# Attention scores with 128 contracted rows: query parts stacked, keys doubled, two matmuls in place of three

## The reference, cut to what matters

```python
C_NA = 1024; NA_HEADS = 16; NA_HEAD_DIM = 64        # 16 heads of 64 channels
scale = dh ** -0.5                                   # 0.125
s_g = jnp.einsum('bhnqd,bhrnkd->bhnqrk', qb, kb).astype(f32) * scale
s_g = s_g + bias.transpose(0, 2, 3, 1, 4)[None]
s_g = jnp.where(mask[:, :, None, :], s_g, NEG_INF)
s_x = jnp.einsum('bhnqd,bhmd->bhnqm', qb, k_m).astype(f32) * scale + mb[None, :, None, None, :]
s = jnp.concatenate([s_g.reshape(B, H, ncb, NA_QB, kh * NA_KU), s_x], axis=-1)
p = jax.nn.softmax(s, axis=-1).astype(v.dtype)
```

## Time and profile before

| what | us |
|---|---|
| median of 3 runs | 1200.71 (1199.37 to 1201.31) |
| profiled execution | 1199.38 |
| its span in the trace | 1197.6 |
| PE busy | 1144.7 (96% of the span) |
| DVE busy | 756.7 (63%) |
| ACT busy | 551.2 (46%) |

### The profile page before, as it was taken

One profiled execution on the slowest core, in us unless ns is written; L12 is line 12 of the kernel. 1 busy time (PEld: TensorE's weight loads), 2 busy tenths in 40 slices (PEclk: granted clock), 3 DMA queues, 4 the chain that ended last, 5 costly groups with the idle time before them and its releaser, 6 DMA issues.

```text
span 1197.6 us, 17295 instructions
## 1 busy us (share of the span) xinstructions
PE 1144.7 (96%) x7254; PEld 1021.8 (85%) x7254; DVE 756.7 (63%) x1118; ACT 551.2 (46%) x750; POOL 65.0 (5%) x100
## 2 busy tenths in 40 slices
PE   4876999999999999999999999999999999999996
PEld 1775999999999999999999988888888888888885
DVE  5755688676786676885768756555455454555553
ACT  6543455445554545554445445444444434444443
POOL 4300001100021000200000000000000000000000
PEclk9987999999999999999999999999999999999998
DMA  8631443543425433344334575555555555556652
GB/s 302 190 103 62 141 141 117 191 159 141 142 106 194 165 123 131 135 147 164 123 141 141 169 257 199 179 205 178 184 203 176 190 197 176 198 189 230 262 180 102
DMA packets 30790, 201.52 MB, mean 168 GB/s; under 512 B 4039, under 2 KB 4360, under 8 KB 8168
## 3 DMA queue, kind: packets, MB, share of 16 engines
q1 hardware_dynamic: 25112, 179.56, 42.7%
q0 software_dynamic: 5312, 19.80, 5.0%
q10 hardware_dynamic: 288, 1.05, 0.2%
HBM read 195.15 MB, written 5.24 MB: 167 GB/s over the span
## 4 chain that ended last, share of the span: by engine, by line
PE 79%; DVE 11%; ACT 6%; issue 3%; DMA 1%; SPq 0%; ACTq 0%; DVEq 0%
PE ps L534 25%; PE ps L536 25%; PE ps L535 25%; DVE w_lo L1219 2%; ACT w_hi L907 2%; PE ps L539 1%; DMA xin<-x 1%; DVE hm L1297 1%; PE ps L560 1%; DVE prod L1470 1%; DVE prod L1471 1%; PE ps L636 1%; PE ps L676 0%; DVE sd L1303 0%; DVE u L1428 0%
## 5 line engine op out<-in xcount | busy, mean ns | idle before, releaser
L1219 DVE TENSOR_TENSOR w_lo<-raw,w_hi 128x1024 fp32r<-128x1024 f32 x336 | 410.0, 1230 | 316.8 <-ACT w_hi L907 315.4
L907 ACT ACTIVATE w_hi<-raw 128x1024 fp32r<-128x1024 f32 x336 | 352.6, 1057 | 406.2 <-PE ps L536 405.4
L534 PE MATMUL ps<-xn_hi,w_hi 128*128 128x272 f32 (+2 forms) x1280 | 369.2, 288 | 1.2 <-issue 1.2
L536 PE MATMUL ps<-xn_hi,w_lo 128*128 128x272 f32 (+2 forms) x1280 | 365.2, 285 | 0.0
L535 PE MATMUL ps<-xn_lo,w_hi 128*128 128x272 f32 (+2 forms) x1280 | 364.9, 285 | 0.0
L534 PEld LDWEIGHTS ps<-xn_hi,w_hi 128*128 128x128 f32 x1280 | 241.8, 189 | 5.9 <-issue 4.6
L536 PEld LDWEIGHTS ps<-xn_hi,w_lo 128*128 128x128 f32 x1280 | 241.7, 189 | 0.0
L535 PEld LDWEIGHTS ps<-xn_lo,w_hi 128*128 128x128 f32 x1280 | 241.7, 189 | 0.0
L534 PE MATMUL ps<-w_hi,xn_hi 128*128 128x512 f32 x384 | 152.2, 396 | 0.0
L536 PE MATMUL ps<-w_hi,xn_lo 128*128 128x512 f32 x384 | 151.0, 393 | 0.0
L535 PE MATMUL ps<-w_lo,xn_hi 128*128 128x512 f32 x384 | 150.6, 392 | 0.0
(11 more groups left out here) (248 smaller groups left out, 1373.0 us busy)
## 6 DMA issues: line engine op xcount, KB each, us to landing
raw<-w_stream SPq DMA_DIRECT2D x168, 1024.0 KB, 4.9
branch_y<-ystage POOLq DMA_DIRECT2D x12, 256.0 KB, 3.3
y_raw<-branch_y POOLq DMA_DIRECT2D x3, 1024.0 KB, 6.9
xin<-x SPq DMA_DIRECT2D x2, 1024.0 KB, 8.2
w4s<-w POOLq DMA_DIRECT2D x16, 128.0 KB, 4.7
absd<-decay POOLq DMA_DIRECT2D x8, 256.0 KB, 6.0
h<-x POOLq DMA_DIRECT2D x2, 1024.0 KB, 8.6
rows_t<-rpb POOLq DMA_DIRECT2D x8, 219.0 KB, 5.2
```

Source lines behind the costliest of these rows:

```text
L534: mm(out_ap, a_hi, b_hi, start=first, stop=False)
L536: return mm(out_ap, a_lo, b_hi, start=False, stop=last)
L907: A(w_hi[:, w % 2, part, :], raw[:, w % 4, 1024 * part:1024 * part + 1024], ACT.Copy).then_inc(hi_done, 1)
L1219: return V.tensor_tensor(dst, src, hi.bitcast(F32), ALU.subtract)
```

## The change

The two parts of a head's query are stacked on the 128 partitions (`q_two`, one slice for each of the four heads of a chunk): the high part stays on the 64 partitions where the projection left it, the low part goes to the other 64. The keys of a head are written twice, to the lower and to the upper 64 partitions, their high part in `k_hi` and their low part in `k_lo`. A matmul of `q_two` against `k_hi` contracts 128 rows and gives both (high + low query) times high key; a second one against `k_lo` gives both times low key. Two matmuls replace three, and the product low times low comes in addition.

The q evacuation becomes four instructions of 64 x 256 on ACT and four on DVE (two and two before). The k evacuation becomes four of 64 x 2 x 272 on ACT and four on DVE (one and one before), and the 16 repeated key columns are copied on each engine from what it has just written, behind a wait for its own last write (before: a second read of PSUM, without a wait). The larger buffers take the place of others: `gate` and `envel` now overlap them, so the gate of step 13 also waits for the chunk's last scores, the high keys wait for the previous chunk's last use of `gate`, and the low keys for the last use of `envel`. The initial buffers `zt`, `mlpw`, `red` and `hid` move too.

```diff
--- before.py
+++ after.py
@@ -199,7 +199,6 @@
     w4_lo = place("w4_lo", [128, 2, CC], F32R)
     w4_hi = place("w4_hi", [128, 2, CC], F32R)
     absd = place("absd", [128, 2, CC])
-    envel = place("envel", [128, 2, 2, CC])
     sd_rest = place("sd_rest", [128, 2, CC], F32R)
     kspec = place("kspec", [128, 2, 3, 2, CC])
     uT_hi = place("uT_hi", [128, 3, CC], F32R)
@@ -229,8 +228,6 @@
     sd = place("sd", [128, 2, CC])
     at[0] = x2_end
     o = place("o", [128, 2, NG])
-    first_at = at[0]
-    gate = place("gate", [128, 2, NG])
     ystage = place("ystage", [128, 2, NG])
     fold_at = at[0]
     folded = place("folded", [128, 2, L])
@@ -244,27 +241,30 @@
 
     p2_hi, p2_lo = (a[:, :, :, :].rearrange("p t r n -> p t (r n)")[:, :, 0:2 * FK] for a in (y_hi, y_lo))
     qk_at = at[0]
-    q_hi = place("q_hi", [128, 2, NG], F32R)
-    q_lo = place("q_lo", [128, 2, NG], F32R)
-    k_hi = place("k_hi", [128, 2, L + NM], F32R)
-    k_lo = place("k_lo", [128, 2, L + NM], F32R)
+    q_two = place("q_two", [128, HC, NG], F32R)
+    k_hi = place("k_hi", [128, HC, L + NM], F32R)
+    k_lo = place("k_lo", [128, HC, L + NM], F32R)
     qk_end = at[0]
     at[0] = qk_at
     fi_hi = place("fi_hi", [128, 2, L], F32R)
     fi_lo = place("fi_lo", [128, 2, L], F32R)
     fi = place("fi", [128, 2, L])
+    gate = place("gate", [128, 2, NG])
+    at[0] += 128
+    envel = place("envel", [128, 2, 2, CC])
+    assert at[0] <= qk_end
     at[0] = qk_end
     u = place("u", [128, 2, L])
     prod = place("prod", [128, 3, 2, CC])
 
     at[0] = xin_at
     xin = place("xin", [128, 3, D])
-    at[0] = first_at
+    at[0] = attn_at
     zt = place("zt", [EMB, L])
     mlpw = place("mlpw", [HID, 3 * HID + 4])
     red = place("red", [HID, 4, L])
-    at[0] = first_at - 4 * 2 * NG
     hid = place("hid", [HID, L])
+    assert at[0] <= attn_end
     at[0] = mix_at
 
     m_hi = place("m_hi", [128, KT, NG], F32R)
@@ -339,6 +339,7 @@
         kx_evac = sem("kx_evac")
         kf_evac = sem("kf_evac")
         k_done = sem("k_done")
+        khi_done = sem("khi_done")
         a_ev = sem("a_ev")
         proj_read = sem("proj_read")
         t_mm = sem("t_mm")
@@ -661,11 +662,11 @@
                 last.then_inc(inv_mm, 1)
 
             def scores(hh):
-                i, r = hh // 2, slice(64 * (hh % 2), 64 * (hh % 2) + 64)
                 for a in range(2):
                     ks = slice(NM, NM + L) if a == 0 else slice(0, L)
-                    last = three(ps[:, 6 + a, 0:L], q_hi[r, i, 128 * a:128 * a + 128], q_lo[r, i, 128 * a:128 * a + 128],
-                                 k_hi[r, i, ks], k_lo[r, i, ks], True, True)
+                    q_both = q_two[:, hh, 128 * a:128 * a + 128]
+                    mm(ps[:, 6 + a, 0:L], q_both, k_hi[:, hh, ks], start=True, stop=False)
+                    last = mm(ps[:, 6 + a, 0:L], q_both, k_lo[:, hh, ks], start=False, stop=True)
                 last.then_inc(s_mm, 1)
 
             def turn_p():
@@ -1070,12 +1071,19 @@
                                 scale=params[:, bass.ds(c * 2 + (CW + 24 + t0 + i), 1)])
                 elif name == "q":
 
-                    for i in range(2):
-                        ins = A(q_hi[:, i, :].rearrange("p (r n) -> p r n", r=4),
-                                ps[:, bank + i, 0:NG].rearrange("p (r n) -> p r n", r=4)[:, :, ::-1], ACT.Copy, scale=0.125)
+                    for hh in range(HC):
+                        r = slice(64 * (hh % 2), 64 * (hh % 2) + 64)
+                        ins = A(q_two[r, hh, :].rearrange("p (r n) -> p r n", r=4),
+                                ps[r, bank + hh // 2, 0:NG].rearrange("p (r n) -> p r n", r=4)[:, :, ::-1], ACT.Copy, scale=0.125)
                 elif name == "k":
-                    A(k_hi[:, :, 0:L], src, ACT.Copy)
-                    ins = A(k_hi[:, :, L:L + NM], ps[:, bank:bank + 2, 0:NM], ACT.Copy)
+                    if c:
+                        act.wait_ge(yb_done, c)
+                    for odd in range(2):
+                        for rows in (0, 64):
+                            ins = A(k_hi[rows:rows + 64, odd:HC:2, 0:L], ps[64 * odd:64 * odd + 64, bank:bank + 2, 0:L], ACT.Copy)
+                    ins.then_inc(khi_done, 1)
+                    act.wait_ge(khi_done, c + 1)
+                    ins = A(k_hi[:, :, L:L + NM], k_hi[:, :, 0:NM].bitcast(F32), ACT.Copy)
                 elif name == "fin":
                     act.wait_ge(fi_done, c + 1)
                     A(fi_hi[:, :, :], fi[:, :, :], ACT.Copy).then_inc(fihi_done, 1)
@@ -1084,6 +1092,8 @@
                     done, turns = {"hgate": (yb_done, c), "ngate": (ya_done, c + 1), "fgate": (yc_done, c + 1)}[name]
                     if turns:
                         act.wait_ge(done, turns)
+                    if name == "hgate":
+                        act.wait_ge(s_mm, c * HC + HC)
                     ins = A(gate[:, :, :], src16, ACT.Tanh, scale=0.5)
                 ins.then_inc(a_ev, 1)
 
@@ -1435,14 +1445,21 @@
                     tap(2, 0, slice(p0, L - 1), slice(1, L - p0))
                     ins = tap(2, 1, slice(p0, L - 1), slice(1, L - p0))
                 elif name == "q":
-                    for i in range(2):
-                        ins = V.scalar_tensor_tensor(q_lo[:, i, :].rearrange("p (r n) -> p r n", r=4),
-                                                     ps[:, bank + i, 0:NG].rearrange("p (r n) -> p r n", r=4)[:, :, ::-1], 0.125,
-                                                     q_hi[:, i, :].rearrange("p (r n) -> p r n", r=4).bitcast(F32),
+                    for hh in range(HC):
+                        r, other = (slice(64 * ((hh + n) % 2), 64 * ((hh + n) % 2) + 64) for n in range(2))
+                        ins = V.scalar_tensor_tensor(q_two[other, hh, :].rearrange("p (r n) -> p r n", r=4),
+                                                     ps[r, bank + hh // 2, 0:NG].rearrange("p (r n) -> p r n", r=4)[:, :, ::-1], 0.125,
+                                                     q_two[r, hh, :].rearrange("p (r n) -> p r n", r=4).bitcast(F32),
                                                      ALU.mult, ALU.subtract)
                 elif name == "k":
-                    lo_part(k_lo[:, :, 0:L], src, k_hi[:, :, 0:L])
-                    ins = lo_part(k_lo[:, :, L:L + NM], ps[:, bank:bank + 2, 0:NM], k_hi[:, :, L:L + NM])
+                    dve.wait_ge(h4_read, 6 * c + 6)
+                    for odd in range(2):
+                        r = slice(64 * odd, 64 * odd + 64)
+                        for rows in (0, 64):
+                            ins = lo_part(k_lo[rows:rows + 64, odd:HC:2, 0:L], ps[r, bank:bank + 2, 0:L],
+                                          k_hi[r, odd:HC:2, 0:L])
+                    link(ins)
+                    ins = V.tensor_copy(k_lo[:, :, L:L + NM], k_lo[:, :, 0:NM].bitcast(F32))
                 elif name == "fin":
                     dve.wait_ge(fihi_done, c + 1)
                     ins = lo_part(fi_lo[:, :, :], fi[:, :, :], fi_hi[:, :, :])
```

## The result

The changed kernel takes 1203.7 us (median of 11 runs, 1203.0 to 1204.6) where the kernel before takes 1200.3 us in the same session (11 runs, 1199.2 to 1201.6). The ratio is 1.0028, with a 95% interval of 1.0020 to 1.0036: slower by 3.4 us. The forecast was 4.7 us faster.

What follows compares the result with a forecast made beforehand. PE sets the pace, with DVE holding it up at one place in every chunk. Gains less losses of 1.42 (chunk 0), 0.93 each (1 and 2) and 1.46 (3) make 4.7 us: 1200.71 to 1196.0, range 1193.3 to 1200.6.

Steps and rivals of the forecast that it cites:

- What PE gains: Scores on PE: two fewer matmuls and free borders give 0.63, 0.63, 0.53, 0.53 us a head, 9.3 us in four chunks.
- Rival 1: Border distances at scores come from the waits in front, not the 64 rows, and stay: 0.4 us faster, 1200.3; chance 0.13.
- Head 3: Chunks 0 to 2: DVE beside POOL holds back what scores(3) saves; PE waits for `o`, 3 x 0.53 = 1.6 us lost.
- The q evacuation: Step 3, chunks 1 to 3: longer evacuation makes `sd_rest` 0.86 us later, PE's wait 1.29 to 2.15, 2.6 us lost.
- four pieces of 64 x 256 cost twice what two of 128 x 256 did: q pieces, length going by elements per partition: +0.54 us on ACT, about +0.67 on DVE.
- Rival 3: Pieces across or within partition halves take half as long again, k becomes the wait: 1.5 us slower, 1202.2; chance 0.06.
- zero for q: Chunk 0, step 3: nothing on PE waits behind the q evacuation in this way, so zero lost; at most another 0.9.
- The k evacuation: Before scores(0) in chunk 0: ACT's +1.7 and DVE's +2.1 us add up, `kspec` 0.46 later, 0.37 us lost on PE.
- the cover of k: Chunks 1 to 3: k_lo ends at 277.9, PE asks at 279.0 + 0.13; slabs 5 and 6 cover it by 1.2 us.
- the rival that came true: Rival 4: clock falls to 0.50 after the 2.15 us waits, three times 2.3 = 7 us, 1202.9; chance 0.05.

Runs made afterwards that it cites:

- the order by half: The changed kernel with the four q pieces of ACT and of DVE in the order of heads 0, 2, 1, 3: 1200.7 us, ratio 1.0005.

## Why the prediction was wrong

**What PE gains: right.** 0.64, 0.64, 0.6 and 0.55 us a head were measured for 0.63, 0.63, 0.53 and 0.53, 9.7 us on PE for 9.3. Rival 1 is out: the borders went with the 64 rows, and went as well when three matmuls were kept. The rule of "TensorEngine Tiling (Array Packing)", Key Properties, in the Trainium skill, that a change of mode drains TensorE, agrees with both runs.

**Head 3: the right size, one place off.** 1.6 us were to be lost in waits for `o`. They were lost about 0.55 us at a time in front of `attend` in step 14, where PE waits for the probabilities; the waits for `o` stayed at 0.8 us in all. The cause is the one given: with POOL's tables out of the way, both waits are gone.

**The q evacuation: the first term that failed.** Step "four pieces of 64 x 256 cost twice what two of 128 x 256 did": 0.86 us a chunk, 1.54 measured. The elements were counted right. What was wrong is that a piece always starts some 0.1 us before the one ahead ends; that didn't hold where the half of the partitions changes. In heads' order each of the four changes halves, so none overlaps: 0.39 us each on ACT, not 0.27, and 0.43 on DVE, not 0.34. The trace of before could have shown it. ACT writes `sd_rest` twice in a row there, to partitions 0 to 15 and then 32 to 47, and a little later `uT_hi` to all 128, to 0 to 15 and to 32 to 47 (timeline of ACT, chunk 1, before):

```profile
255.67 0.63 ACT L973 ACTIVATE sd_rest<-sd 16x512 fp32r<-16x512 f32 x1 [1.72 <-DVE sd L1303]
256.31 0.63 ACT L974 ACTIVATE sd_rest<-sd 16x512 fp32r<-16x512 f32 x1
...
257.51 0.61 ACT L1092 ACTIVATE uT_hi<-ps 128x512 fp32r<-128x512 f32 x1
257.99 0.36 ACT L1093 ACTIVATE uT_hi<-ps 16x256 fp32r<-16x256 f32 x1
258.36 0.38 ACT L1094 ACTIVATE uT_hi<-ps 16x256 fp32r<-16x256 f32 x1
```

The two of `sd_rest` are 0.64 us apart at a duration of 0.63: no overlap. From 128 partitions to the first 16 of them there is one, 0.13 us; on to partition 32 there is none. So these rows and the q pieces agree with a start partition that must stay the same, not the whole range. I took my distance from instructions that keep theirs. The Trainium skill, "ScalarE: Activation LUTs", What ACT_TABLE_LOAD costs, says that ACTIVATEs back to back overlap by about 93 ns. The whole pieces of before agree with that (0.11 us), the four new ones in heads' order don't, and the measurement decides. Rival 3 had pieces that take half as long again, 1.2 us more a chunk where 0.68 came; but its reason, writing across the halves, was not it, since in the order by half every one of DVE's pieces still reads and writes what it did, and they overlap where two in a row keep their partitions. In chunk 0, where the prediction had zero for q, the long wait for `sd_rest` grew by 0.3 us; by half it didn't.

**The k evacuation: mis-sized in chunk 0.** 0.37 us predicted, a wait of 1.7 measured, of which about 1.0 is the change's. DVE, chunk 0, after, and PE's first score (beside the earlier trace rows):

```profile
112.20 2.93 DVE L1229 TENSOR_TENSOR k_lo<-ps,k_hi 64x544 fp32r<-64x544 f32 x4 [4.22 <-ACT k_hi L1086]
115.16 0.20 DVE L1462 CAST k_lo<-k_lo 128x64 fp32r<-128x64 f32 x1
115.39 0.68 DVE L1487 TENSOR_TENSOR prod<-ps,kspec 16x512 f32<-16x512 f32 x1
...
120.22 0.69 DVE L1332 TENSOR_TENSOR kspec<-kspec,ps 128x512 f32<-128x512 f32 x1
...
121.01 0.36 PE L668 MATMUL ps<-k_hi,q_two 128*128 128x272 f32 x1 [1.51 <-issue]
```

The four pieces take 2.93 us where 2.56 were reckoned, ACT's four 2.50 for 2.0: the same missing overlap. Counted from the start of the filter matmuls, `kspec` is 1.2 us later, where I had 0.46. The end of `kspec` at 120.91 releases the first score at 121.01. The rest of the 1.7 is that PE itself came to the place 0.6 us earlier (12.4 us after them, before 13.1), since the clock came back sooner in this execution (4.4 us behind the restart, before 5.8). The kernels with the same k evacuation took 13.0 to 13.2 us there in the other traces, so the change doesn't cause that. In chunks 1 to 3 the cover of k held, as predicted, also in the kernels where the clock stayed at 1.00. The run with `both_bins` ahead of the k evacuation has no wait there in chunk 0 either.

**The clock: the rival that came true, at a chance of 0.05.** The prediction put the point "between 1.3 and 7 us, and 2.15 is near the lower end" and took that for safety. Between the ends nothing was known, and a wait of 1.76 us was enough in one case of three. It cost 5.7 us in the profiled run, 1.5 to 2.7 a time. This step decided the sign. With the q and k terms corrected and the clock left alone, the sum would have been 4.7 - 3 x 0.68 - 0.3 (q in chunk 0) - 0.7 (k) = 1.7 us faster, within what can't be told from no change.

**What the traces leave open.** Why the clock fell behind every wait in the changed kernel, behind two of three in one kernel with waits of 2.7 us, and behind one of three in another with 2.8. The executions of the changed kernel agree within 1.6 us, those of the other two differ by 5 to 6 us. Where in time the waits fall may matter, and so may the chip, which wasn't the same in all sections; neither was tested. The rule of the start partition is read from rows, and only the order of the q pieces was changed to test it.

## What to carry to other kernels

Where one engine sets the pace, first list the places where it already waits, and cost what a change adds to the other engines there and nowhere else. Here 9.7 us saved were outweighed by evacuations that put 1.5 us in front of the one wait of each chunk, and moving one piece of DVE's work out of its way brought the changed kernel from 3.4 us slower to 6 us faster, 4 of them the move's own. A short pause on TensorE can cost nearly its length again through the clock: 1.5 to 2.7 us behind 10 of the 15 profiled waits of 1.76 to 2.85 us. When an evacuation is cut into pieces by partitions, do those of one partition range one after the other, and count the full duration of a piece wherever the range changes. Compare a repaired kernel with the kernel before under the same repair, or the repair's gain is counted as the change's.

## What the runs showed of the hardware

- A block of 64-row tiles between tiles of 128 costs about 0.09 to 0.11 us at each of four starts around it, three where tiles of 16 columns follow: 5.0 us over 16 blocks. A tile of 80 rows between tiles of 128 shows nothing of the kind (0.12 and 0.13 us around it in `attend`).
- ACT and DVE start an instruction about 0.1 us before the one ahead ends where both begin at the same partition, and wait for its end at the changes of partition looked at here: 1.31 against 1.55 us for the same four pieces in two orders on ACT, 1.53 against 1.73 on DVE.
- The granted clock fell from 1.00 to 0.50 behind 10 of 15 waits of 1.76 to 2.85 us, behind none of nine of 1.3 us in the profiled runs. One fall costs 1.5 us, and 2.7 in one case.
- POOL's additions slow DVE beside them: two weight splits take 3.10 instead of 2.35 us, the scaling of the probabilities 1.79 instead of 0.63. With POOL's work moved away, the same instructions of the same chunk take 2.35 and 0.63.
